# GpSimd subtracts the low parts of all streamed weights, one unit after the other, in place of VectorE

## What is computed

```
for l in range(2):                       # first network
    hx = modulate(rms_norm(x, norm1_g[l]), sh1, sc1)
    px = hx @ w_in[l]
    x = x + g1 * (concat(attention, fourier, hyena) @ w_out[l])
    x = x + g2 * (square(relu(modulate(rms_norm(x, ...)) @ w_mlp1[l])) @ w_mlp2[l])
for layer in range(2):                   # second network
    y = hgrn2_mixer(u, ...)  or  dilated_attention_mixer(u, ...)
    h = h + (1 + g1) * rms_norm(y, ...)
    y = swiglu_ffn(modulated rms_norm(h), ffn_w_in[layer], ffn_w_out[layer])
    h = h + (1 + g2) * rms_norm(y, ...)
```

## Time and profile before

| what | value |
|---|---|
| median of 3 runs | 4082.75 us (4079.91 to 4088.29) |
| profiled execution | 4088.66 us |
| its span, first to last instruction | 4086.5 us |
| mean granted TensorE clock | 0.94 of full speed |
| PE busy | 3695.5 us, 90% |
| DVE busy | 1896.1 us, 46% |
| ACT busy | 1344.1 us, 33% |
| POOL busy | 4.3 us, 12 instructions |

### The profile page before, as it was taken

The page is one execution under the profiler, slowest core; times in us unless marked ns, Lnnn a source line. Parts: engine busy times, 40 slices in busy tenths (PEclk is TensorE's granted clock), DMA queues, the critical chain, the costliest instruction groups (busy, mean ns, idle before and its releaser), DMA issues. The chain is left out here.

```text
span 4086.5 us, 43975 instructions
## 1 busy us (share of the span) xinstructions
PE 3695.5 (90%) x18416; PEld 3026.3 (74%) x18416; DVE 1896.1 (46%) x2938; ACT 1344.1 (33%) x1846; POOL 4.3 (0%) x12
## 2 busy tenths in 40 slices
PE   7969898899999999788986799699969999968998
PEld 6768555788888755587775677688858888867887
DVE  2221544455555444456664555433345454543333
ACT  1021234433223423352223544522253332344223
POOL 0000000000000000000000000000000000000000
PEclk9859999999999999998998899799979999989999
DMA  5321300133333230146661221132214232312321
GB/s 188 108 85 44 103 11 1 62 106 103 118 114 109 62 98 0 42 147 215 205 225 36 73 62 62 42 103 93 93 37 103 66 89 66 96 45 69 101 95 52
DMA packets 415524, 360.73 MB, mean 88 GB/s; under 512 B 64815, under 2 KB 410078, under 8 KB 413919
## 3 DMA queue, kind: packets, MB, share of 16 engines
q1 hardware_dynamic: 415327, 357.92, 28.3%
HBM read 350.02 MB, written 4.72 MB: 87 GB/s over the span
## 5 line engine op out<-in xcount | busy, mean ns | idle before, releaser
L381 PE MATMUL ps<-second_h_hi,second_w_hi 128*128 128x512 f32 (+1 forms) x1776 | 685.7, 386 | 76.0 <-DVE second_h_lo L603 47.4
L381 PE MATMUL ps<-second_h_lo,second_w_hi 128*128 128x512 f32 (+1 forms) x1776 | 667.1, 376 | 0.0
L381 PE MATMUL ps<-second_h_hi,second_w_lo 128*128 128x512 f32 (+1 forms) x1776 | 666.2, 375 | 0.0
L453 DVE TENSOR_TENSOR second_w_lo<-ring,second_w_hi 128x2048 fp32r<-128x2048 f32 (+2 forms) x140 | 290.7, 2077 | 439.2 <-ACT second_w_hi L405 439.2
L381 PE MATMUL ps<-h_mix_hi,w_hi 128*128 128x512 f32 (+1 forms) x1192 | 424.1, 356 | 47.1 <-DVE h_mix_lo L603 23.7
L381 PEld LDWEIGHTS ps<-second_h_hi,second_w_hi 128*128 128x128 f32 x1776 | 347.8, 196 | 136.7 <-issue 54.7
L381 PE MATMUL ps<-h_mix_lo,w_hi 128*128 128x512 f32 (+1 forms) x1192 | 417.5, 350 | 0.0
L381 PE MATMUL ps<-h_mix_hi,w_lo 128*128 128x512 f32 (+1 forms) x1192 | 416.4, 349 | 0.0
L381 PEld LDWEIGHTS ps<-second_h_lo,second_w_hi 128*128 128x128 f32 x1776 | 348.2, 196 | 56.0 <-issue 1.7
L381 PEld LDWEIGHTS ps<-second_h_hi,second_w_lo 128*128 128x128 f32 x1776 | 346.5, 195 | 57.8
L405 ACT ACTIVATE second_w_hi<-ring 128x2048 fp32r<-128x2048 f32 (+2 forms) x140 | 242.8, 1735 | 237.6 <-PE ps L381 227.8
(11 more groups left out here) (349 smaller groups left out, 5538.9 us busy)
## 6 DMA issues: line engine op xcount, KB each, us to landing
ring<-in_w_mlp SPq DMA_DIRECT2D x64, 1024.0 KB, 5.4
side_w<-in_ada_w SPq DMA_DIRECT2D x96, 512.0 KB, 4.8
ring<-in_ffn_w_in SPq DMA_DIRECT2D x44, 1024.0 KB, 5.0
wm<-in_w_mod SPq DMA_DIRECT2D x24, 1024.0 KB, 5.4
side_w<-in_w_mod SPq DMA_DIRECT2D x48, 512.0 KB, 3.6
ring<-in_attn_w_in SPq DMA_DIRECT2D x48, 512.0 KB, 5.1
ring<-in_hgrn_w_in SPq DMA_DIRECT2D x32, 512.0 KB, 5.5
ring<-in_ffn_w_out SPq DMA_DIRECT2D x16, 1024.0 KB, 5.1
```

The costliest lines, as they stand in the source:

```text
L381: mm = pe.matmul(acc, lhsT, rhs, start=k == 0 and wp == ap, stop=k == j.kt - 1 and wp == 1)
L453: dve.tensor_tensor(unit.place(unit.slot[1]), unit.place(M.ring[:, u % RING, :]), unit.place(unit.slot[0]), ALU.subtract).then_inc(*S.w_lo ...
```

## The change

The call of `low` leaves `Region.vector` and goes to a new GpSimd list that holds nothing else: one subtraction for each unit, in the units' order. The instruction, its operands and its wait for the high part stay; who waits for it (TensorE at the unit's first job, SyncE ahead of the fetch of unit u+2) stays too.

```diff
-    def low(self, dve, u):
+    def low(self, pool, u):
         S, M, unit = self.S, self.M, self.units[u]
-        dve.wait_ge(S.w_hi.sem, S.w_hi.at(u + 1))
-        dve.tensor_tensor(unit.place(unit.slot[1]), unit.place(M.ring[:, u % RING, :]), unit.place(unit.slot[0]),
+        pool.wait_ge(S.w_hi.sem, S.w_hi.at(u + 1))
+        pool.tensor_tensor(unit.place(unit.slot[1]), unit.place(M.ring[:, u % RING, :]), unit.place(unit.slot[0]),
                           ALU.subtract).then_inc(*S.w_lo.one)
     def vector(self, dve):
         S, M = self.S, self.M
-        u = 0
-        while u < len(self.units) and self.freed(u) < 0:
-            self.low(dve, u)
-            u += 1
         yield -1
...
-            while u < len(self.units) and self.freed(u) <= j.at:
-                self.low(dve, u)
-                u += 1
             yield j.at
+
+    def gpsimd(self, pool):
+        for u in range(len(self.units)):
+            self.low(pool, u)
...
+            @block.gpsimd
+            def _(pool):
+                self.gpsimd(pool)
```

## The result

The changed kernel takes 4111.6 us (median of 6 executions, 4109.4 to 4114.6) where the kernel before, on the same chip, takes 4088.0 (median of 6). The ratio is 1.0059, 95% interval 1.0046 to 1.0072: 24 us slower.

What follows compares the result with a forecast made beforehand. TensorE, busy 90% of the span, was taken as the bound, so VectorE's relief counts only where TensorE waits. Terms 14.4 + 8.1 + 17 - 4 - 15 - 1.9 = +18.6 on 4082.75 gave 4101 us, range 4057 to 4150.

Steps and rivals of the forecast that it cites:

- likeliest case: The forecast itself: GpSimd subtractions of 4.5 us taking turns with two-input VectorE instructions; +18.6 us, 4101 us, chance 0.48.
- Part 1, small margins: Two stage starts, five border units and five more whose low part has under 2.2 us to spare: +14.4 us.
- Part 2, `SplitThread` starts: Starts at unit 50 and in the stage of units 7 to 49 come later behind longer subtractions: +4.4 and +3.7.
- Part 3, side columns: Two-input side products wait for GpSimd's turn, so `mods` comes 1.3 us later; 12 such waits and some new: +17.
- Part 4, the recurrence: The `r_qs` product ends about 0.5 after GpSimd, 0.5 us earlier than before, in each of 8 heads: -4.
- Parts 5 and 6, borders and the end: Second network's border reduces and copies start earlier, less L664 held: -15; two evacuations behind unit 191 come earlier: -1.9.
- The rival "VectorE is not held": Two-input VectorE instructions do not wait for a running GpSimd one, everywhere: -63 us, 4020 us; chance 0.10.
- The length of the subtraction: GpSimd subtraction assumed 4.5 us; rivals: shorter, 3.5 gives -16 (chance 0.12); longer, 5.2 gives +43, 6.4 +85 (chance 0.16).

Runs made afterwards that it cites:

- The run with these units alone: Only units 57 to 85 have their subtraction on GpSimd, against the kernel before: ratio 1.0037 (1.0020 to 1.0054), +15 us.
- the long zero writes: Changed kernel with each GpSimd subtraction replaced by zeros written two and a half times over the same buffer: 4029.4 us, ratio 0.9861 to the kernel before.
- The run with five units: Only units 107, 108, 141, 193 and 194 have their subtraction on GpSimd, against the kernel before: 4070.2 us, ratio 0.9953.

## Why the prediction was right

The sign, the size and the mechanism held: +18.6 forecast, +24 measured (interval 19 to 29), inside the likeliest case's own range of 4085 to 4125. Of the 10.6 us between 4101 and 4111.6, 5.3 are the base: the kernel before has 4088.0 in the six executions beside it and 4082.75 in the three that the forecast starts from. By the prediction's parts, from the start of each unit's first matmul in the two traces (shift: how much later it starts in the changed kernel, us; `end` is the span's end):

```
unit        0     50     56     57     86    105    106    140    190    192    end
shift    +9.2  +21.2  +26.3  +30.8  +37.5  +42.2  +36.0  +32.0  +30.1  +23.2  +23.4
```

- **Part 1, small margins (+14.4).** The five border units moved as said: 10 by +1.9, 42 by +1.8, 105 by +1.9, 142 by about +1, 190 by +1.6. Unit 86's start was +2.2 in the run in which the second network alone moved. The other five gave nothing: unit 11 comes 2.1 later, and 12 makes that up (-2.2); 43 and 44 likewise. So this term was about 2 too large.
- **Part 2, `SplitThread` starts (+4.4 and +3.7).** The step at unit 50 is +4.4 and at unit 8 is +3.8. Its price was too small in what follows it: from unit 50 to 56 the shift grows by 5.1 more, for which no term stood. Windows around the wait ahead of unit 50 and the two at and behind the start of unit 54, first of the kernel before, then of the changed one (length; busy us of PE, PEld, DVE, ACT, POOL; granted clock, DMA share, GB/s):

```profile
1710.00:1725.00 15.00, 12.25 (x47) 10.04 (x48) 7.57 (x10) 4.47 (x9) 0.00 (x0) 0.79 0.23 73
1765.00:1780.00 15.00, 13.69 (x103) 13.44 (x103) 8.11 (x11) 10.35 (x15) 0.00 (x0) 0.92 0.38 119
```

```profile
1731.00:1747.00 16.00, 13.04 (x45) 10.58 (x46) 7.78 (x9) 2.46 (x5) 2.27 (x1) 0.72 0.21 67
1788.00:1806.00 18.00, 15.47 (x102) 15.08 (x103) 12.62 (x10) 10.41 (x15) 9.20 (x2) 0.82 0.25 73
```

  The granted clock fell from 0.79 to 0.72 and from 0.92 to 0.82, for about as many matmuls. The wait ahead of unit 50 grew from 15.2 to 19.6 us, and the two at unit 54 from 3.92 to 4.96 and from 1.31 to 2.53, by 2.3 in sum; behind each the engine worked longer at the lower clock. With the two waits taken off, 2.8 us of the 5.1 are left; 1.15 of them lie between the first matmuls of units 50 and 51, where TensorE waits in neither kernel. The prediction priced the wait at unit 50 alone.
- **Part 3, side columns (+17).** The run with these units alone gives +15 (8 to 22). The place near 1929 us grew by 0.86, not 1.3, but there are 15 waits in place of 12. And one wait of another kind, which the prediction doesn't have, grew from 2.7 to 7.7 us: ahead of unit 57, on `side_a`, where three and then eight side products stand beside two subtractions in a row (unit 57 comes 4.5 later):

```profile
1825.55 5.68 DVE L772 SCALAR_TENSOR_TENSOR side_a<-side_w,cond,side_a 128x256 f32<-128x256 f32 x3
1831.16 0.41 DVE L470 TENSOR_TENSOR hid_lo<-f,hid_hi 128x256 fp32r<-128x256 f32 x1
1831.49 7.49 DVE L772 SCALAR_TENSOR_TENSOR side_a<-side_w,cond,side_a 128x256 f32<-128x256 f32 x8
...
1839.03 0.59 PE L751 MATMUL ps<-ones,side_a 128*128 128x1 f32 x2 [7.73 <-DVE side_a L772]
```

  The sum was about right, its make-up was not: fewer us per wait, and a wait at the head of the stage. The `mods` and `side_a` waits together are 9.5 us longer; where the rest of the 15 lies is not shown.
- **Part 4, the recurrence (-4).** Seven of the eight waits on `r_qs` fell from 2.42 to about 2.1, which is -0.3 each; the first rose from 3.6 to 4.4. Together -1.5, in place of -4. From unit 89 to 104 the shift falls by 0.6 here, by 11.2 with the subtraction in four pieces and by 18.1 with the long zero writes. Timeline of one head (the one ahead of that of the earlier trace rows):

```profile
2423.96 4.58 POOL L453 TENSOR_TENSOR second_w_lo<-ring,second_w_hi 128x2048 fp32r<-128x2048 f32 x1 [12.59 <-ACT second_w_hi L405]
...
2426.62 2.47 DVE L1929 TENSOR_TENSOR r_qs<-r_qs,r_eb 128x512 f32<-128x512 f32 x1
...
2429.14 1.25 PE L1827 MATMUL ps<-r_qs,r_nb 128*128 128x128 f32 x5 [2.12 <-DVE r_qs L1929]
```

  L1929 ends at 2429.09, 0.55 after GpSimd, as the prediction had it. The mechanism held; its margin of 0.5 us a head was small enough for a subtraction of 4.58 in place of 4.5 and the first head's loss to eat most of it.
- **Parts 5 and 6, borders and the end (-15 and -1.9).** From unit 105 to the end the shift falls by 18.8, with -6.2 at 106, -4.1 from 106 to 140 and -6.9 from 190 to 192. With units 142 and 190 of part 1 taken in, the terms give -14, so the gain was about 5 larger than priced. The run with five units shows the first two steps without L664 being held: -7.2 and -3.3 (-5.8 from 190 to 192).
- **The rival "VectorE is not held".** It was priced at -63, and the long zero writes, in which the held side products and `r_qs` run free, gave -57. So its price was right in sum and its condition false. By parts the writes gave -18.1 in the recurrence (priced -17.6), -26 from unit 56 to 86 (priced -40 for the side columns) and -24.5 from unit 105 on (priced -20), so the sum is closer than its parts. The one place of 0.12 us in the earlier trace rows pointed the right way, though it was thin evidence.
- **The length of the subtraction.** The 4.5 us were a choice between 3.25 and 6.4. It is 4.64 in the median; by the prediction's own 35 us for each us that is +5, an estimate (it is contained in the parts above). Had it been 3.5 or 5.2, the sign or the size would have failed with every mechanism right.

The total is closer than its parts. Against the prediction's terms, parts 2 and 4 came out about 5 and 2.5 us worse, and parts 1, 3, 5 and 6 about 2, 2 and 5 us better: that these nearly cancel is luck. With the measured parts the sum would be about 17, so some 7 us of the timed +24 (19 to 29) stand in no term, and what they are stays open.

The Trainium skill, SBUF — State Buffer, section "Who interferes with whom", says a VectorE instruction with two inputs in SBUF excludes only a GpSimd one that reads SBUF, while a TENSOR_SCALAR that runs in a two-port mode contends with any. The runs agree: under GpSimd's zero writes the side products of L779 keep their 478 ns, under its subtractions their means are 620 and 603, and the TENSOR_SCALAR of L776 is held by both (up to 1977 ns under the writes, up to 4703 under the subtractions). Whether it runs in such a mode no run here shows. The subtraction takes 4.49 us at the least, which agrees with the 4497 ns that the Trainium skill gives for a GpSimd add of 2048 fp32 elements (GPSIMD Engine Reference, section 3.1).

Two things qualify this. The shift of 9.2 us at unit 0 holds only 2.2 of the change; the other 7 arose in the opening, which the change doesn't touch. Over the profiled executions of all kernels unit 0 starts from 8.9 us earlier to 9.6 us later than in the profile of before, in no order with what GpSimd does (+7.1 with only units 57 to 85 moved, -8.9 with only the second network moved). And kernels whose units 57 to 85 are untouched go from 57 to 85 between 0.5 and 9.9 us faster than that profile does. So +23.4 in the profile and +24 by the medians agree partly by chance; the timed ratios of the runs carry the verdicts, the traces carry the places.

## What to carry to other kernels

Work moved from VectorE to an idle GpSimd can cost VectorE the moved work's whole length, wherever an operation that excludes it is due meanwhile. Ask of each operation beside it how many inputs it reads from SBUF, and move only those pieces that stand ahead of something TensorE waits for and beside one-input work; but the one-input TENSOR_SCALAR was held here, too, so look at the durations in the trace. Here that was five of 226: -19 us (by the ratio) in place of +24. A wait's price isn't its length alone: add the matmuls behind it at the lower clock. And where a kernel has two parts of different make, time a move in each by itself, since the sum hides a gain and a loss.

## What the runs showed of the hardware

- A GpSimd subtraction of 128x2048 to fp32r takes 4.49 us at the least, 4.64 in the median and 5.48 at the most, beside VectorE's 2.29. Pieces of 128x512 take 1.30 us in the median and 1.25 at the least, so four of them take longer (5.2 us) than one of 128x2048. GpSimd, too, is held: the subtraction at 2651.33 us takes 5.32, with VectorE's two-input `second_h_lo` running from 2649.83 to 2652.18.
- GpSimd's zero write takes 1.8 us for 2048 columns, and it holds VectorE's TENSOR_SCALAR (348 ns alone, up to 1977), not its SCALAR_TENSOR_TENSOR (486 ns at the most of 672).
- With the same instructions the opening differs by up to 18 us between profiles. Windows from 150 to 200 us, first of the run on the second network (unit 0 at 294 us), then of the run on units 0 to 56 (unit 0 at 312 us):

```profile
150.00:200.00 50.00, 50.00 (x301) 43.40 (x301) 12.10 (x19) 3.72 (x7) 0.00 (x0) 0.92 0.43 133
```

```profile
150.00:200.00 50.00, 50.00 (x252) 42.22 (x250) 10.52 (x19) 3.83 (x7) 0.00 (x0) 0.80 0.34 106
```

  TensorE is busy throughout both, at a granted clock of 0.92 and of 0.80: the first does 301 matmuls where the other does 252. When it falls from the 2.4 GHz level to the 1.2 GHz one differs from run to run. What decides it stays open.
